# State-space decays: the backward diagonal arguments made in PSUM by TensorE, the forward ones by VectorE, with four decay banks

## What is computed

```
y[t] = sum over s of  (C[t] . B[s]) * ( F[s,t] + G[s,t] ) * x[s]
F[s,t] = exp(cum_f[t] - cum_f[s] + log dt_f[s])   for s <= t, else 0      (forward, inclusive)
G[s,t] = exp(cum_b[t] - cum_b[s] + log dt_b[s])   for s >  t, else 0      (backward, strict)
```

## Time and profile before

| | |
|---|---|
| median of three runs | 1483.41 us |
| the profiled execution's own time | 1481.16 us |
| its span, first to last instruction | 1479.4 us |
| mean granted TensorE clock | 0.997 |
| TensorE matmuls busy | 1414.8 us, 96% |
| VectorE busy | 812.6 us, 55% |
| ScalarE busy | 658.7 us, 45% |
| GpSimd busy | 833.4 us, 56% |

### The profile page before, as it was taken

How to read it: one execution, slowest core, us unless ns; L and a number is a source line. 1 busy time by engine, 2 the same in 40 slices (tenths; PEclk the granted TensorE clock), 3 DMA queues, 4 the chain that set the end, 5 groups by cost and what they waited for, 6 DMA issues and landing times.

```text
span 1479.4 us, 22770 instructions
## 1 busy us (share of the span) xinstructions
PE 1414.8 (96%) x8868; PEld 1204.8 (81%) x8868; DVE 812.6 (55%) x1581; ACT 658.7 (45%) x1069; POOL 833.4 (56%) x670
## 2 busy tenths in 40 slices
PE   5989989999999999889999999999999999999997
PEld 3968788999987887645878888888888956999997
DVE  3687678777566678578674433321136667422211
ACT  3446665554543232774342232232236376544442
POOL 1523507999874443574445545545436620799985
PEclk9999999999999999999999999999999999999999
DMA  9656705777784662110545555533333320466564
GB/s 367 252 186 242 264 12 203 263 249 251 229 275 173 207 194 71 43 44 1 185 149 193 199 199 183 194 125 93 96 100 116 114 85 1 132 197 186 182 184 119
DMA packets 71323, 242.59 MB, mean 164 GB/s; under 512 B 7473, under 2 KB 13105, under 8 KB 70833
## 3 DMA queue, kind: packets, MB, share of 16 engines
q1 hardware_dynamic: 68800, 237.15, 47.8%
q10 hardware_dynamic: 2416, 4.00, 0.9%
HBM read 239.02 MB, written 1.05 MB: 162 GB/s over the span
## 4 chain that ended last, share of the span: by engine, by line
PE 50%; DVE 4%; ACT 2%; POOL 1%; issue 1%; DMA 0%; DVEq 0%; ACTq 0%; POOLq 0%
PE bank L555 15%; PE bank L557 15%; PE bank L556 15%; PE bank L994 1%; PE cond_a L994 1%; DVE h_lo L2061 1%; PE bank L1002 1%; PE cond_a L1054 1%; PE bank L1014 1%; PE cond_b L1014 1%; PE cond_b L1002 0%; ACT w_hi L1328 0%; DVE scratch L2662 0%; DVE work L2052 0%; DVE arena L2626 0%
## 5 line engine op out<-in xcount | busy, mean ns | idle before, releaser
L1847 POOL TENSOR_TENSOR w_lo<-raw,w_hi 128x512 fp32r<-128x512 f32 (+1 forms) x612 | 773.6, 1290 | 605.5 <-ACT w_hi L1328 594.0
L1328 ACT ACTIVATE w_hi<-raw 128x1024 fp32r<-128x1024 f32 (+3 forms) x301 | 308.8, 1029 | 585.6 <-PE bank L557 518.0
L555 PE MATMUL bank<-h_hi,w_hi 128*128 128x256 f32 (+2 forms) x1604 | 525.8, 328 | 9.1 <-DVE h_lo L1928 2.6
L557 PE MATMUL bank<-h_hi,w_lo 128*128 128x256 f32 (+2 forms) x1604 | 521.5, 325 | 0.0
L556 PE MATMUL bank<-h_lo,w_hi 128*128 128x256 f32 (+2 forms) x1604 | 521.5, 325 | 0.0
L555 PEld LDWEIGHTS bank<-h_hi,w_hi 128*128 128x128 f32 (+1 forms) x1604 | 301.6, 188 | 44.1 <-DVE h_lo L1928 5.8
L557 PEld LDWEIGHTS bank<-h_hi,w_lo 128*128 128x128 f32 (+1 forms) x1604 | 301.6, 188 | 26.7
L556 PEld LDWEIGHTS bank<-h_lo,w_hi 128*128 128x128 f32 (+1 forms) x1604 | 301.8, 188 | 25.5
L555 PE MATMUL bank<-hidden_hi,w_hi 128*128 128x256 f32 (+1 forms) x528 | 167.6, 317 | 0.3 <-POOL w_lo L1847 0.2
L556 PE MATMUL bank<-hidden_lo,w_hi 128*128 128x256 f32 (+1 forms) x528 | 167.2, 317 | 0.0
L557 PE MATMUL bank<-hidden_hi,w_lo 128*128 128x256 f32 (+1 forms) x528 | 167.2, 317 | 0.0
(11 more groups left out here) (426 smaller groups left out, 1749.7 us busy)
## 6 DMA issues: line engine op xcount, KB each, us to landing
raw<-in_up SPq DMA_DIRECT2D x132, 512.0 KB, 3.5
ada_w<-in_ada SPq DMA_DIRECT2D x128, 512.0 KB, 4.5
raw<-in_down SPq DMA_DIRECT2D x48, 448.0 KB, 3.4
raw<-in_out SPq DMA_DIRECT2D x24, 512.0 KB, 3.6
raw<-in_down SPq DMA_DIRECT2D x24, 512.0 KB, 3.5
raw<-in_in SPq DMA_DIRECT2D x24, 512.0 KB, 3.6
arena<-in_ada SPq DMA_DIRECT2D x16, 512.0 KB, 11.7
raw<-in_uq SPq DMA_DIRECT2D x12, 384.0 KB, 3.0
```

The lines of the kernel that those rows point to most:

```text
L555: pe.matmul(out, w_h, x_h, start=first, stop=False)
L557: return pe.matmul(out, w_l, x_h, start=False, stop=last)
L1328: act.activation(part_slot(w_hi, f, u), raw_slot(f, u), ACT.Copy).then_inc(s["rounded"], 1)
L1847: pool.tensor_tensor(part_slot(w_lo, f, u)[:, a:b], raw_slot(f, u)[:, a:b], part_slot(w_hi, f, u)[:, a:b].bitcast(F32), ALU.subtract).then ...
```

## The change

Even q is now the backward direction, odd q the forward one (`side_of`), and bank 6 joins 3, 4 and 7, so that a head's two banks alternate with the next head's. The backward diagonal blocks no longer pass VectorE: ScalarE's `backward(h)` exponentiates the pieces off the diagonal right after the spread; then TensorE's `diagonal(h)` writes the whole bank anew with three matmuls that accumulate: the spread, the bias (`bias_rows`, the transposed backward `ngs` as high and low rows, times `own`, which picks the head), and the mask (the identity times `behind`, both rounded copies that ScalarE makes once). `backward_diagonal(h)` exponentiates the blocks from PSUM. VectorE keeps the forward blocks, and before the retention part makes `own` and `bias_rows`. `ssd_weighted` and `group_spread` have bank 5 alone. In `ret_weighted(3)`, `ssd_weighted(1)` and `ssd_weighted(2)` a `diagonal` stands between the first token tile and the rest. The hand-written orders of TensorE, ScalarE, GpSimd and VectorE are redone around this.

The core of the diff (declarations, repeated waits and lists of pieces that stay as they were are left out):

```diff
...
+exact_ident, behind = (work_r[:, 2, i * P:(i + 1) * P] for i in range(2))
+own = work_r[:, 2, 2 * P:2 * P + TT * RH]
...
-sq_r = [sq_sum[:, :], work[:, 2, :], sq_2, scratch[:, 0:512]]
+sq_r = [sq_sum[:, :], sq_1, sq_2, scratch[:, 0:512]]
...
-    return (bank[3], bank[4], bank[7])[q % 3]
+    return (bank[3], bank[4], bank[6], bank[7])[q % 4]
+def side_of(q):
+    return q // 2, 1 - q % 2
+def spread_after(q):
+    return q - 4 if q % 2 else q - 2
...
-            weighted(p, xt, s["sd_y"], 5, s["sd_o"], ea)
+            if p:
+                pe.wait_ge(s["sd_y"], p)
+            weighted(p, xt, bank[5], s["sd_o"], ea, between)
         def spread(q):
-            h, d = divmod(q, 2)
-            if q >= 3:
-                pe.wait_ge(s["sd_e"], q - 2)
+            h, d = side_of(q)
+            if q >= 4:
+                pe.wait_ge(s["sd_e"], spread_after(q))
             pe.matmul(decay_bank(q)[:, :], picks[0:40, h:h + 1].to_broadcast([40, P]), grow[0:40, d, :],
                       start=True, stop=True).then_inc(s["sd_b"], 1)
+        def diagonal(h):
+            pe.wait_ge(s["sd_apart"], h + 3)
+            out = decay_bank(2 * h).rearrange("p (i t) -> p i t", i=TT)
+            mine = own[0:64, :].rearrange("p (i h) -> p i h", i=TT)[:, :, h]
+            pe.matmul(decay_bank(2 * h), picks[0:40, h:h + 1].to_broadcast([40, P]), grow[0:40, 1, :],
+                      start=True, stop=False)
+            pe.matmul(out, bias_rows, mine.unsqueeze(2).to_broadcast([64, TT, P]), start=False, stop=False)
+            pe.matmul(out, exact_ident, behind.unsqueeze(1).to_broadcast([P, TT, P]),
+                      start=False, stop=True).then_inc(s["sd_masked"], 1)
...
+            if i:
+                pe.wait_ge(s["gn_done"], i)
             for t in range(TT):
...
+        for n in (64, 96):
+            last = pe.matmul(bank[6][n:n + 32, 0:P], sums_flat[:, 96:128], ident, start=True, stop=True)
...
                 spread(1)
-            ret_weighted(p)
-        group_sums(2)
+                pe.wait_ge(s["rt_y"], 3)
+                spread(2)
+            ret_weighted(p, (lambda: diagonal(0)) if p == 3 else None)
+        ssd_scores(0, 0)
         pe.wait_ge(s["rt_y"], 4)
-        spread(2)
         spread(3)
-        ssd_scores(0, 0)
-        spread(4)
-        group_sums(3).then_inc(s["gn_sum"], 1)
+        diagonal(1)
         ssd_scores(0, 1)
         ssd_scores(0, 2)
+        spread(4)
         spread(5)
+        group_sums(2)
+        group_sums(3).then_inc(s["gn_sum"], 1)
+        diagonal(2)
+        spread(6)
+        pe.wait_ge(s["sd_e"], 3)
+        idle(bank[7], 3 * P, 3 * P)
+        spread(7)
         pe.wait_ge(s["gn_inv"], 1)
         group_spread(0)
-        spread(6)
         group_spread(1)
-        spread(7)
+        diagonal(3)
         group_spread(2)
         spread(8)
+        spread(9)
         group_spread(3)
-        pe.wait_ge(s["gn_done"], 3)
+        diagonal(4)
+        pe.wait_ge(s["gn_done"], 4)
         ssd_weighted(0)
-        spread(9)
         spread(10)
-        pe.wait_ge(s["gn_done"], 4)
-        idle(bank[6], 3 * P, 3 * P)
         spread(11)
-        idle(bank[6], 3 * P, 3 * P)
+        ssd_scores(1, 0)
+        diagonal(5)
+        ssd_scores(1, 1)
+        ssd_scores(1, 2)
         spread(12)
-        for i in range(3):
-            ssd_scores(1, i)
         spread(13)
-        ssd_weighted(1)
+        ssd_weighted(1, lambda: diagonal(6))
         spread(14)
         spread(15)
-        pe.wait_ge(s["sd_y"], 1)
-        idle(bank[5], 3 * P, 3 * P, 3 * P, 3 * P)
-        ssd_weighted(2)
+        ssd_weighted(2, lambda: diagonal(7))
+        pe.wait_ge(s["sd_y"], 3)
+        idle(bank[5], 3 * P, 3 * P, 3 * P)
         def rest(k):
             if k == 0:
-                pe.wait_ge(s["sd_e"], 2 * RH)
-                idle(bank[3], 3 * P, 3 * P, 3 * P)
                 ssd_weighted(3)
             if k == 2:
...
     round_next()
-    def ssd_decays(q):
-        h, d = divmod(q, 2)
-        total, e = ea[h % 5], eb[h % 2] if d else ea[h % 5]
-        act.wait_ge(s["sd_arg"], q + 1)
+    def apart(q):
+        h, d = side_of(q)
+        total, e = ea[h % 5], eb[h % 2]
+        act.wait_ge(s["sd_b"], q + 1)
         g = decay_bank(q)
...
+        for out, i, t0, t1_ in pieces:
+            last = act.activation(out, g[:, t0:t1_], ACT.Exp, bias=ngs[:, d, i, h:h + 1])
+        return last
+    def backward(h):
+        if h == 0:
+            act.wait_ge(s["rt_p"], 12)
+        if h == 1:
+            act.wait_ge(s["rt_o"], 4)
+        if h >= 2:
+            act.wait_ge(s["sd_sum"], h - 1)
...
+        apart(2 * h).then_inc(s["sd_apart"], 1)
+    def forward(h):
+        act.wait_ge(s["sd_arg"], h + 1)
+        apart(2 * h + 1)
         for lat in range(2):
-            near = triangles(e, lat)
+            near = triangles(ea[h % 5], lat)
             last = act.activation(near, near, ACT.Exp)
+        last.then_inc(s["sd_e"], 1)
+    def backward_diagonal(h):
+        act.wait_ge(s["sd_masked"], h + 1)
+        blocks = decay_bank(2 * h).rearrange("p (i t) -> p i t", i=TT)
+        for lat in range(2):
+            last = act.activation(triangles(eb[h % 2], lat), blocks[:, 2 * lat:2 * lat + 2, :], ACT.Exp)
         last.then_inc(s["sd_e"], 1)
     def ret_squares(p):
...
     for p in range(3):
         ret_squares(p)
-    for q in range(3):
-        ssd_decays(q)
-        if q == 1:
+    act.wait_ge(s["tables_in"], 32)
+    for out, table in ((exact_ident, ident), (behind, C1("behind"))):
+        act.activation(out, table, ACT.Copy).then_inc(s["sd_apart"], 1)
+    for h in range(2):
+        backward(h)
+        if h == 1:
             ret_squares(3)
+        forward(h)
+        backward_diagonal(h)
+    backward(2)
...
-    for q in range(3, 2 * RH):
-        ssd_decays(q)
+    for h in range(2, RH):
+        if h > 2:
+            backward(h)
+        forward(h)
+        backward_diagonal(h)
...
-        if h in (4, 6):
-            gate_product(h // 2 - 2)
-        if h == 6:
-            square_sum(0)
+        if h in (3, 4):
+            round_group(h - 3)
+        if h == 5:
+            round_group(2)
+            gate_product(0)
+            round_group(3)
+    gate_product(1)
+    square_sum(0)
     square_sum(1)
...
         copy(grow[0:40, 0, :], bank[6][0:40, :])
+        copy(bias_rows, bank[6][64:128, 0:P])
         then(copy(grow[0:40, 1, :], bank[7][0:40, :]))
...
+        def decay_arguments(h):
...
-            dve.wait_ge(s["sd_b"], q + 1)
-            g = decay_bank(q)
-            mask = C1("behind" if d else "ahead")
+            dve.wait_ge(s["sd_b"], 2 * h + 2)
+            g = decay_bank(2 * h + 1)
             for i in range(TT):
                 last = dve.scalar_tensor_tensor(out=triangle(e, i), in0=g[:, i * P:(i + 1) * P],
-                                                scalar=ngs[:, d, i, h:h + 1], in1=mask,
+                                                scalar=ngs[:, 0, i, h:h + 1], in1=C1("ahead"),
                                                 op0=ALU.add, op1=ALU.add)
             last.then_inc(s["sd_arg"], 1)
...
                 keep_ret(p - 1)
         decay_arguments(0)
+        keep_ret(3)
         decay_arguments(1)
...
         ssd_weigh(0)
+        decay_arguments(2)
         dve.wait_ge(s["gn_std"], 1)
         dve.reciprocal(gn_inv, gn_inv).then_inc(s["gn_inv"], 1)
-        decay_arguments(5)
+        decay_arguments(3)
         scale_group(0)
-        decay_arguments(6)
+        ssd_weigh(1)
         scale_group(1)
-        decay_arguments(7)
-        ssd_weigh(1)
         scale_group(2)
-        decay_arguments(8)
+        decay_arguments(4)
         scale_group(3)
         dve.wait_ge(s["gn_done"], 4)
         for k in range(4):
             dve.nop().then_inc(s["h_work"], 1)
-        decay_arguments(9)
         ssd_weigh(2)
+        ssd_weigh(3)
+        decay_arguments(5)
         gate_ssd(0)
-        decay_arguments(10)
-        decay_arguments(11)
-        ssd_weigh(3)
-        decay_arguments(12)
-        decay_arguments(13)
         ssd_weigh(4)
+        decay_arguments(6)
+        ssd_weigh(5)
         gate_ssd(1)
-        decay_arguments(14)
-        decay_arguments(15)
-        ssd_weigh(5)
+        decay_arguments(7)
         lower(0)
+        lower(1)
         ssd_weigh(6)
+        gate_ssd(2)
+        lower(2)
         ssd_weigh(7)
-        gate_ssd(2)
-        lower(1)
-        lower(2)
         gate_ssd(3)
...
```

68 lines of the change are left out of this document (33 added, 35 removed).

## The result

The changed kernel takes 1494.17 us (median of nine runs, 1489.63 to 1497.08); the kernel before took 1485.63 on the same chip (nine runs, 1478.55 to 1490.04). The ratio is 1.006, with an interval of 1.0042 to 1.0077: about 8.5 us slower, just over the 0.5% that was to count. The forecast was no change, +2.5 us, with a range of 1479 to 1493; the result lies 1.2 us above it.

A forecast was written before the change was run, and what follows sets the result against it. In the changed part, queues waiting on one another were taken as the bound, not TensorE's own work. +5.0 (a to d), -4.2 (e), +1.0 (f) and +0.7 (g) gave +2.5 on 1483.4: 1485.9 us, range 1479 to 1493.

The forecast's parts named there:

- (f): TensorE's clock: high up to ssd_weighted(0), perhaps falling at the waits just ahead of ssd_weighted(3); +1.0 us, up to 2.7.
- (e): From ssd_weighted(0) to ssd_weighted(3): VectorE has four blocks less, GpSimd is late next; 23.9 us for 28.1, -4.2.
- (a): Ahead of the retention part: added VectorE and TensorE preparation, partly swallowed by a GpSimd wait; +0.7 us, bounds 0 and 1.2.
- (b): diagonal(0) in the middle of ret_weighted(3): TensorE waits 1.0 us, the diagonal takes 0.8; rt_o 4 comes +2.7 us.
- (c): Group norm behind ret_weighted(3): ScalarE ends the square root at 647.3 us, the reciprocal comes at 647.7, +3.9 us.
- (d): group_spread with one bank: turns of 1.9 us no longer overlap; ssd_weighted(0) at 657.5 us instead of 652.50, +5.0.
- (g): Correction to the whole walk, since waits between engines are a little longer than the 0.05 us assumed; +0.7 us.
- Rival 1: VectorE is the bound all along in the changed part and its 8.3 us come off: 1475.1 us; chance 0.07.
- Rival 2: The diagonal's turn between TensorE and ScalarE stands bare, 2.5 us in each of heads 5 to 7: 1493.4; chance 0.09.
- Rival 3: Clock high at the end and (a) swallowed, 1484.2; or falling ahead of ssd_weighted(0) and at the end, 1489.3; chance 0.15 together.
- Rival 4: Queue order in (d) loses less than walked, +2 to +3 against -4.2: 1482 us or so; chance 0.1.
- The signs: Forecast wrong if ssd_weighted(0) starts before 655 us, or TensorE's waits for ScalarE inside weighted products pass 1 us each.

The follow-up runs named there:

- e6: e5 plus two idle matmuls ahead of ret_scores(1); ratio 1.0061 to the kernel before.
- e10: Changed kernel with idle matmuls only: two ahead of ret_scores(1), one ahead of diagonal(0), and those of e1; ratio 1.0047 to the kernel before.
- e12: Changed kernel with GpSimd's squares waiting until all four gated products are there; ratio 1.0108 to the kernel before.
- e1: Changed kernel with four and eight idle matmuls, instead of three, around the last waits ahead of ssd_weighted(3); 1494.44 us, ratio 1.0069 to the kernel before.
- e14: e12 plus the idle matmuls of e10 and two more ahead of group_sums(2); ratio 1.0124 to the kernel before.
- e9: e6 with two idle matmuls put back ahead of the reciprocal's wait; median 1495.39 us, ratio 1.0072 to the kernel before.
- e7: Kernel before with GpSimd's round_group(2), round_group(3), gate_product(1) and square_sum(0) behind all heads' additions; 1489.98 us, ratio 1.0033 to the kernel before.
- e8: Changed kernel with VectorE making its block of forward arguments twice for h = 4 to 7; ratio 1.0094 to the kernel before.
- e4: Changed kernel with GpSimd's round_group(2) and (3) behind all heads' additions and lower(2) behind ssd_weigh(7); 1488.17 us, ratio 1.003 to the kernel before.
- e15: Changed kernel with the four roundings on ScalarE, diagonal(0) later, group_spread first, lower(2) behind ssd_weigh(7), and idle matmuls; ratio 1.0052 to the kernel before.
- e5: Changed kernel with the edits of e1 and e4, diagonal(0) behind ret_weighted(3), and group_spread first without its idle matmuls; ratio 1.0042 to the kernel before.

## Why the prediction was wrong

Held against the forecast's own points, the 7.6 us between 96.8 and 104.35 fall into four pieces: 3.0 up to the square root, 0.8 from there to `ssd_weighted(0)`, 2.4 to `ssd_weighted(3)`, 1.4 behind it. Two steps of the sum carry nearly all of it: (f), the clock, and (e), VectorE's operations at the end.

- **(a) Prep, +0.7: right.** `keep_ret(2)` comes 0.58 us later than before once the clock is kept up (29.75 against 29.17 in e6 and e10). What I left out is that TensorE waits 2.17 us there, for 1.58 before, and that its clock falls afterwards, which it didn't before; the same point is 1.7 later in the changed kernel.
- **(b), (c) The diagonal in `ret_weighted(3)` and the square root behind it: right in kind and, at full clock, in size.** e10: 6.1 us between the two `keep_ret` (forecast 5.8), the square root at 43.6 (43.4). The diagonal's stop was 0.74 us for 1.0, its matmuls 1.08 at full clock for 0.8. At the granted clock the square root came at 46.3. So 2.7 of the 3.0 us are **step (f)**.
- **(d) Group norm in one bank, +5.0 up to `ssd_weighted(0)`: the mechanism was right, 0.8 too little behind the square root.** The first group spread started 2.45 us after the square root's end for 1.9, and from it to `ssd_weighted(0)` it took 8.6 us for 8.3. The rows show why. TensorE gets to the first group spread through `diagonal(2)`, `spread(6)`, two idle matmuls and `spread(7)`, which take 1.08, 0.43, 1.48 and 0.43 us from start to start, 3.4 in all, where I had 0.8, 0.33, 1.4 and 0.33, 2.9 in all. And `ssd_weighted(0)` starts right behind `diagonal(4)` (664.87 to 665.94), 0.3 us after VectorE's last `scale_group` has ended, and not behind that one as I had it. So I had the diagonal and the spreads too short. I had put the diagonal's second and third matmul at 0.23 us, the distance of out1's, and each spread at 0.33, the distance of two of them.
- **(e) 23.9 us between the weighted products: mis-sized.** GpSimd was late, as said, and ended its seven steps 0.6 us behind the walk. I gave VectorE's product, lower(2) and far addition 0.6 to 1.1 us, the durations of before, where GpSimd's work lay differently beside them. They took 1.5 to 1.7 beside GpSimd's squares; e12, which moves only those squares, takes 2.8 us off the stretch. This is the term that was mis-sized. With the 0.7 of (g) the forecast had 24.6; e12 has 24.2.
- **(f) The clock: the step that failed.** I took it as high up to `ssd_weighted(0)`, since the walk showed waits of 0.3 to 1.1 us only, and set 1.0 us at the end. It cost 2.7 ahead of the square root (e10) and 2.4 at the end (e1). How much of the 2.7 counts at the end is less sure: in e10 the clock fell again in the group norm and took it back, and with the clock up throughout (e14) `ssd_weighted(0)` was 1.5 us earlier, the added idle matmuls included. What such a fall can cost is seen best between e6 and e9, which differ in two idle matmuls: `ssd_weighted(0)` at 60.2 and at 54.3. Between the two weighted products it cost nothing (26.96 us at 0.90 and at 1.00). And the 1.7 us that `ssd_weighted(0)` lost before were no gain to be had: in e7, with the clock up, the next product came no earlier.
- **Rival 1**, VectorE as the bound: wrong; of the 4.1 us that e8 puts back 2.1 reach `ssd_weighted(3)`, and `ssd_weighted(0)` came 8.8 us later than before. What e4 and e15 win in the stretch behind it holds `lower(2)` too.
- **Rival 2**, the diagonal's stops bare: the stops inside the weighted products are 0.74, 0.29 and about 0, far from the 2 us a head from which it was to decide. Its number, 1493.4, was met by luck, for other reasons.
- **Rival 3** came nearest: the clock, at the end and ahead of `ssd_weighted(0)`. But it put the early fall at that product, which ran at full clock; the fall that cost lay ahead of the square root. Its upper case, 1489.3, took the cost of one product at each place, where the falls also lengthened what lay around them.
- **Rival 4**, less lost in (d): wrong, with `ssd_weighted(0)` 8.8 us later for 5.0.
- **The signs.** Neither sign of being wrong came: `ssd_weighted(0)` wasn't early and TensorE's waits in the products stayed under 1 us. Both looked for the queues, and none for the clock. `ssd_weighted(0)` at 57.4 us, for 53.6, was the sign that did come.
- **The page against a row.** I set exponentials out of PSUM at 0.04 us more than out of SBUF, from two rows of different operands. The changed kernel has both with the same operands:

```profile
L1781 ACT ACTIVATE arena<-arena 128x256 f32<-128x256 f32 x8 | 3.0, 448 | 0.0
L1781 ACT ACTIVATE scratch<-scratch 128x256 f32<-128x256 f32 x8 | 2.9, 423 | 0.0
L1789 ACT ACTIVATE arena<-cond_b 128x256 f32<-128x256 f32 x8 | 2.7, 401 | 0.0
L1789 ACT ACTIVATE arena<-cond_a 128x256 f32<-128x256 f32 x8 | 2.6, 390 | 0.1
```

Out of PSUM (cond_a, cond_b) they are 0.02 to 0.06 us cheaper. The Trainium skill (VectorE: DVE Perf Modes, section The TRN2 errata) said so, by 52 cycles each. These rows agree with it, and I was wrong to set it aside: the rows that I had compared differed in the bias operand too. It changes the sum by 0.2 us at most.

What stays open is whether the runs without a trace lose their time in the same stretches. No run shows how much of the 8.5 us between the medians is the clock's. The mean clock of a whole run doesn't carry it: at 0.987 the kernel of before took 1483.0 to 1488.7 us (four runs, over all rounds), the changed kernel 1495.2 and 1496.1. Of the versions with more idle matmuls, e1 and e9 have no lower median than the changed kernel, and e10's, 4.1 us under it, is within the scatter. No version of the change that I ran beats the kernel of before: the best part is 97.3 us against 94.3, the best median 1488.17 (e4). e9's 97.3 still holds the idle matmuls that were late themselves, 25.4 us between the products for e4's 22.05. With fewer of them e9 was not run.

## What to carry to other kernels

Where small or narrow matmuls and short waits take the place of an engine's other work, set TensorE's clock as a cost of its own, at the half rate over the whole stretch that follows as far as TensorE's queue is what the others wait for, and not only where a long wait is seen. Durations of VectorE's operations with two SBUF inputs hold only beside the GpSimd work that they were measured with: when an order moves, look at what now lies beside them. Idle matmuls that fill a wait become the wait once its cause is gone; set their number last.

## What the runs showed of the hardware

- **VectorE and GpSimd hold each other up at SBUF.** The same product takes 0.69 us alone and 1.53 and 1.76 beside a GpSimd operation of 1.03 and 1.27. Each of VectorE's three long operations ends 0.55 us after the GpSimd operation that ran when it started (686.24 + 1.03 is 687.27, and 686.29 + 1.53 is 687.82). Operations with one input in PSUM keep their time beside the same work (L2718 0.74, L2734 1.88 for three, as in e12 with GpSimd idle). GpSimd pays too: its far addition takes 1.72 instead of 1.27 beside VectorE's `lower` operations. The Trainium skill (SBUF — State Buffer, section SBUF: two separate sides) says that the two share a pair of ports which one instruction holds to its end, for VectorE when both its inputs are in SBUF; by this rule, both traces and e12 agree. GpSimd's rounding copies don't fit it: in e4 two of them run from 679.87 to 682.97, and VectorE's product beside them takes 1.10 us, its far addition 0.68 as if alone. The measurement decides: here the copies cost VectorE 0.4 us at most.
- **TensorE's granted clock falls though the engine is busy.** In e5 it was at 0.51, close to the lower level of 1.2 GHz, over 15.2 us in which it was busy for 14.2, with spreads of 40 rows and 128x128 matmuls, and it fell after 6 us and more without a stop. With two idle matmuls of 384 columns ahead of them (e9) it was at 1.00 over the same work, and with more of them earlier (e10) it fell there again, to 0.78. So where it falls can't be told from the waits alone.
- **The clock goes with the scatter.** In several kernels the time follows the mean granted clock: e15's twelve runs go from 1488 us at 0.994 to 1504 us at 0.983, e10's from 1486 at 0.996 to 1499 at 0.985. In others it does so loosely: the changed kernel took 1494.2 at 0.993 and 1489.6 at 0.991. A profile is one such run, and may be the best of them (e9).
